# Hybrid decoder step on one core: fourteen input projections of the mixers as three products of rounded high and low parts, and the first tile's mixing moved forward

## The chip, the core and the metric

The kernel runs on one NeuronCore of one Trainium2 chip. The metric is the device time of one execution in microseconds, median of several runs; the kernel before has a median of 2032.25 us. The five engines are TensorE (PE in the profile, its weight loads PEld), VectorE (DVE), ScalarE (ACT), GpSimd (POOL) and SyncE (SP), which here only issues DMAs.

## What is computed

One inference step of a one-layer decoder on T = 592 tokens (16 meta tokens, 512 prompt tokens, 8 sample sequences of 8 tokens), all in float32. Cut to what matters here:

```python
q, k, v, g, f_lr, z, xbc, dt_raw = jnp.split(rmsnorm(h) @ w_in, offs, axis=-1)
gk   = log_sigmoid(f_lr @ w_gk2 + b_gk2) / 16          # decay of the linear attention
attn = jnp.sum(q[:, :, :, None] * exp(b_t - b_s) * k[:, :, None], axis=-1)   # inside chunks of 16
o    = attn @ v + (q * exp(b)) @ state                  # states follow each other, chunk by chunk
o_gla = rmsnorm(o) * silu(g)
xs, bm, cm = split(silu(causal_conv(xbc)))              # second mixer: state space, 8 heads
y    = rmsnorm((ssd(xs, dt, bm, cm) + d_skip * xs) * silu(z))
h    = h + concat(o_gla, y) @ w_out
h    = h + peer(rmsnorm(h))                             # 16384 experts, product keys, top 16 of 8 heads
```

## The kernel before, in words

Activations lie transposed, features on the 128 partitions and tokens along the row. The program is written out by hand, engine by engine; each engine runs its own list in order and waits on semaphores. There is no scheduler: the order in the source is the order on the engine.

**The mixers (the first 480 us or so).** `project(n, xn)` (L569) multiplies the n-th 128-feature block of `w_in` by the normed activations `xn`: 8 contraction tiles by 2 halves of 296 tokens, so 16 float32 matmuls. Blocks 0 and 1 are q, 2 and 3 are k, 4 to 7 are g, 8 to 11 are z, 12 to 19 are the convolution's input. A block's weights come by DMA into one of four slots of `ring` (`load_w`, L429), each load released when the product that held the slot is done (semaphore `proj_done`); behind each of the loads 4 to 11 SP also issues four 768 KB stores of zeros into the scratch table of gates. ACT copies each product from PSUM (`from_pair`, L1035, semaphore `proj_act`).

The PE runs products 0 to 3, turns k (L647), runs products 4 and 5, and then ten attention units u (two per token tile). A unit is `attn(u, 6 + u)`: sixteen steps, each one matmul of product 6 + u and one matmul with two columns (L662) that sums the decayed q times k over its features. Each unit's input `E_unit[u % 3]` is made by four engines in turn: DVE `decay_arg(u)` (L1387, L1388: difference of the running decays, capped at 0; it waits until unit u - 3 has been used), ACT `decay(u)` (L1073: exp), POOL a product with q (L1790), DVE `mult_k(u)` (L1394: times k), and then the PE. On ACT the exps stand between the copies of the products, with a table load at each change between exp and silu. In unit u DVE does `mult_k(u + 1)`, `decay_arg(u + 3)`, and after each odd unit `attn_matrix` (L385). ACT does, for n = 5 to 11, `from_pair(n)` and then `decay(n - 2)`.

After the units come the chunk-by-chunk states of the linear attention with products 15 to 19 between them, the state-space mixer (`pre`, L765 to L773, on the PE; `decays` L1499 and L1502, `weighted_x` L1511 to L1516 and `mixing` L1523 on DVE; then the outputs L824 on the PE), and the output projections.

**The experts (from about 484 us to the end).** 128 blocks of expert inputs and then 128 of expert outputs, each float32 operand split into a rounded high part and a low remainder in the type fp32r, which the PE takes in one pass: `split_product` (L875) multiplies high by high, high by low and low by high. ACT rounds (L1184), DVE subtracts (L1609).

Of the kernel before, what the change touches and what calls it, by code (L numbers as in the profile page):

```python
# [26 lines left out]
P = 128  # L27
# [19 lines left out]
N_PROJ = N_FEAT + KT + PH  # L47
GRP = 8
# [103 lines left out]
def build(nc, d, o):  # L152

    base = ExitStack()
    with base:
# [9 lines left out]

        h = sb(base, "h", [P, KT, T])
# [8 lines left out]
        prm = sb(base, "prm", [P, PARAM_N])  # L175
        sq = sb(base, "sq", [P, 2, T])
# [20 lines left out]
        mix_stack = ExitStack()  # L197
        mix = sb(mix_stack, "mix", [P, 8, T])
# [22 lines left out]
        khat = sb(gla, "khat", [P, TILES, GH * DK])  # L221
        tmp = sb(gla, "tmp", [P, 2, TILES, GH * DK])
        MT = sb(gla, "MT", [P, TILES, GH * P])
        S = sb(gla, "S", [P, 2, NP, DV])
        Ssm = sb(gla, "Ssm", [P, NSEQ, NP, DV])
# [9 lines left out]
        wv_sb = Ef[:, 0:KT * GH * DV].rearrange("p (k n) -> p k n", k=KT)  # L235
        gsq = Ef[:, 0:GH * T].rearrange("p (h t) -> p h t", h=GH)
# [178 lines left out]
        def _(sp):  # L415
# [26 lines left out]
            sp.dma_start(Ssm[:, :, :, :], d["s_gla"]).then_inc(sgla_loaded, 16)  # L442
            for n in range(12, N_FEAT):
                load_w(n)

# [65 lines left out]
            sp.wait_ge(xl_ready, KT)  # L511
# [38 lines left out]
        def _(pe):  # L550
# [85 lines left out]
            pe.wait_ge(v_copied, 4)  # L636
            project(0, xn, norm=0)
            pe.wait_ge(v_copied, TILES)
            pe.wait_ge(suf_exp, 3)
            for n in range(1, 4):  # L640
                project(n, xn)
# [8 lines left out]
            def attn(u, n=None):  # L650


                i, p = u // 2, u % 2
                if p == 0 and i >= 2:
                    pe.wait_ge(mt_ready, i - 1)
                pe.wait_ge(e_k, u + 1)
                src = E_unit[u % 3][:, 0:rows(i) * C].rearrange("p (t n) -> p t n", t=C)
                for t in range(C):
                    if n is not None:
                        project(n, xn, first=t, count=1)  # L660
                    out = bank[4 + i % 2][0:rows(i), p * 2 * C + t:p * 2 * C + C + t + 1:C]
                    mm = pe.matmul(out, src[:, t, :], cc("head2"), start=True, stop=True)  # L662
                mm.then_inc(attn_used, 1)


            project(4, xn)
            project(5, xn)
# [199 lines left out]
            def split_product(b, x, first=False):  # L867

                for k in range(KT):
                    if first:  # L870
                        pe.wait_ge(xl_ready, k + 1)
                    hi, lo = (usp[:, x, z, k * P:(k + 1) * P] for z in range(2))
                    for w, src in ((hi, xh), (hi, xl), (lo, xh)):
                        for y in range(2):
                            mm = pe.matmul(bank[b + y][:, 0:PHALF], w, src[:, k, y * PHALF:(y + 1) * PHALF],  # L875
                                           start=(k == 0 and w is hi and src is xh), stop=(k == KT - 1 and w is lo))
                return mm
# [24 lines left out]

            for n in range(N_FEAT + KT + 1, N_PROJ):
                pe.wait_ge(qlo_ready, n - N_FEAT - KT)
                wait_proj_evacuated(pe, n)
                split_product(2 * (n % 2), n % NU, n == N_FEAT + KT + 1).then_inc(proj_done, 1)
                if n == N_FEAT + KT + 1:
                    pe.wait_ge(hsm_keys_loaded, 32)
                if n >= N_FEAT + KT + 2:
                    first_scores(n - N_FEAT - KT - 2)  # L910
# [99 lines left out]
        def _(act):  # L1010
# [43 lines left out]
            act.wait_ge(rtok_ready, 2)  # L1054
            for i in range(TILES):
                act.wait_ge(v_done, i + 1)
                act.activation(V[0:rows(i), i, :], bank[[2, 3, 0, 1, 2][i]][0:rows(i), :], ACT.Copy,
                               scale=rtok[0:rows(i), i:i + 1]).then_inc(v_copied, 1)
# [16 lines left out]
            for n in range(15):  # L1075
                if n < 4:
                    from_pair(n, (qT if n < 2 else kT)[:, n % 2, :], scale=(DK ** -0.5 if n < 2 else 1.0))
                elif n < 12:
                    from_pair(n, (sg if n < 8 else sz)[:, n % 4, :], ACT.Silu)
                else:  # L1080
                    from_pair(n, h[:, n - 12, :])
                if n < 3:
# [219 lines left out]
        def _(dve):  # L1302
# [72 lines left out]
            dve.tensor_scalar(gk[:, :, :], tmp[:, 1, :, :], 1.0 / 16.0, None, ALU.mult).then_inc(gk_ready, 1)  # L1375
            dve.wait_ge(b_copied, 4)
# [19 lines left out]

            for u in range(3):
# [9 lines left out]

            dve.wait_ge(proj_act, 4)
            dve.wait_ge(khat_step, 1)
# [6 lines left out]
            mult_k(0)  # L1416
            for u in range(2 * TILES):
                if u + 1 < 2 * TILES:
                    mult_k(u + 1)
                if u + 3 < 2 * TILES:  # L1420
                    decay_arg(u + 3)
                if u % 2 == 1:
# [123 lines left out]
            for i in range(TILES):  # L1546
                r = rows(i)
                if i < 4:
                    decays(i + 1)
                mixing(i)  # L1550
# [32 lines left out]
            def low_x(k):  # L1583
                dve.wait_ge(xh_ready, k + 1)
# [197 lines left out]
        def _(pool):  # L1782
# [39 lines left out]
            for n in range(N_FEAT + KT + 1, N_PROJ):  # L1822
                pool.wait_ge(qhi_ready, n - N_FEAT - KT)
                if n == N_FEAT + KT + 3:
                    pool.wait_ge(xl_ready, KT)
# [124 lines left out]
```

## Time and profile before

| | |
|---|---|
| median of 3 runs (2029.19 to 2039.9) | 2032.25 us |
| the profiled execution | 2029.9 us |
| its span, first to last instruction | 2028.1 us |
| PE busy | 1991.8 us, 98% |
| DVE / ACT / POOL busy | 60% / 31% / 56% |
| mean granted PE clock, share of full speed | 0.988 |

The page gives, for one execution, the busy time of each engine, the chain of work that ended last, and groups of instructions by source line. The timeline lists an engine's instructions in order of start, neighbours of one kind merged: start in us, duration, engine, line, operation, output<-inputs, sizes, count, and in brackets how long the engine stood idle before and what released it. A float32 matmul shows as two records. Durations of matmuls reach from entry to drained result and overlap; the pitch from one start to the next is what a stream costs.

### The profile page before, as it was taken

Reading aid. Unit: us, or ns where it says so; the run is one execution under the profiler, and the core shown is the slowest. Engines: PE = TensorE matmul, PEld = TensorE weight load, DVE = VectorE, ACT = ScalarE, POOL = GpSimd, SP = SyncE. Lnnn points to the kernel's source line nnn. Section 1 sums busy time; section 2 is a strip of 40 time slices with the busy share of each in tenths; the row PEclk is TensorE's granted clock in tenths of the full one; section 3 lists DMA queues with packets and bytes.
Section 4 is the critical chain, followed back from the end, with each engine's and each line's share of the span. In section 5 each row is a group of like instructions: output and inputs, shape, how many; then the busy total and the mean of one; then the engine's idle time right before and its main releaser. Section 6 shows DMA issues by size and latency. Waiting matters only on the chain.

```text
span 2028.1 us, 31741 instructions
## 1 busy us (share of the span) xinstructions
PE 1991.8 (98%) x12557; PEld 1830.1 (90%) x12557; DVE 1216.5 (60%) x2243; ACT 633.6 (31%) x999; POOL 1138.3 (56%) x694
## 2 busy tenths in 40 slices
PE   8999999999999999999999999999999999999997
PEld 4678777868999999999999999998999999999996
DVE  4425365646898877788244331114677777777775
ACT  3325113323333233232323333223333333333332
POOL 0114210222367888888888888885566666666310
PEclk8999999899999999999999999999999999999999
DMA  3395103032245555555555555778999999999971
GB/s 151 108 337 198 32 32 89 1 111 101 96 122 122 130 115 130 121 129 127 127 130 126 120 124 121 171 169 281 333 328 325 326 329 325 326 325 328 330 259 48
DMA packets 233452, 365.28 MB, mean 180 GB/s; under 512 B 92129, under 2 KB 158194, under 8 KB 232690
## 3 DMA queue, kind: packets, MB, share of 16 engines
q1 hardware_dynamic: 154354, 294.37, 43.7%
q0 software_dynamic: 77824, 67.41, 17.0%
q10 hardware_dynamic: 1152, 1.84, 0.3%
q8 instruction: 81, 1.33, 0.3%
q14 instruction: 41, 0.34, 0.0%
HBM read 290.15 MB, written 73.38 MB: 179 GB/s over the span
## 4 chain that ended last, share of the span: by engine, by line
PE 95%; DVE 2%; ACT 1%; DMA 1%; SPq 0%; issue 0%; ACTq 0%; POOL 0%; DVEq 0%; POOLq 0%
PE bank L875 41%; PE bank L992 31%; PE bank L569 9%; PE bank L589 2%; PE bank L797 2%; PE bank L845 2%; PE bank L691 1%; PE bank L555 1%; PE bank L662 1%; PE bank L707 1%; PE bank L922 1%; PE bank L785 1%; PE bank L953 1%; PE bank L831 1%; DMA ring<-in_v 1%; PE bank L765 0%
## 5 line engine op out<-in xcount | busy, mean ns | idle before, releaser
L875 PE MATMUL bank<-xh,usp 128*128 128x288 f32 x4320 | 755.9, 296 | 1.4 <-DVE xl L1585 1.4
L1842 POOL DMA_INDIRECT gates_scratch<-gate_val,gate_at x384 | 674.1, 1755 | 132.6 <-issue 116.1
L875 PEld LDWEIGHTS bank<-xh,usp 128*128 128x128 f32 x4320 | 636.8, 189 | 4.0 <-DVE xl L1585 2.6
L992 PE MATMUL bank<-W,vsp 128*128 128x448 f32 x3072 | 623.1, 365 | 3.2 <-DVE W L1724 3.2
L992 PEld LDWEIGHTS bank<-W,vsp 128*128 128x128 f32 x3072 | 576.8, 188 | 49.1 <-issue 3.5
L875 PE MATMUL bank<-xl,usp 128*128 128x288 f32 x2160 | 462.5, 296 | 0.0
L875 PEld LDWEIGHTS bank<-xl,usp 128*128 128x128 f32 x2160 | 348.0, 189 | 0.0
L1609 DVE TENSOR_TENSOR usp<-ring,usp 128x1024 fp32r<-128x1024 f32 x120 | 146.6, 1221 | 335.1 <-ACT usp L1184 334.8
L1719 DVE TENSOR_TENSOR vsp<-ring,vsp 128x1024 fp32r<-128x1024 f32 x128 | 157.0, 1226 | 179.2 <-ACT vsp L1266 179.2
L1207 ACT ACTIVATE gl<-bank 128x288 f32<-128x288 f32 x256 | 91.3, 409 | 523.9 <-PE bank L875 523.8
L1861 POOL DMA_INDIRECT picked<-in_v,row_index x128 | 149.4, 1167 | 182.9 <-DVE acc L1738 162.4
L1868 POOL DMA_INDIRECT hid_b<-hidden_scratch,hid_index x128 | 190.1, 1485 | 55.3 <-issue 38.7
L569 PE MATMUL bank<-xn,ring 128*128 128x296 f32 x640 | 202.8, 439 | 0.0
L1266 ACT ACTIVATE vsp<-ring 128x1024 fp32r<-128x1024 f32 x128 | 135.6, 1060 | 183.3 <-PE bank L992 168.7
L1738 DVE SCALAR_TENSOR_TENSOR acc<-picked,w_b,acc 128x1024 f32<-128x1024 f32 x126 | 160.3, 1278 | 0.2
L1270 ACT ACTIVATE W<-sq 128x448 fp32r<-128x448 f32 x128 | 74.2, 580 | 233.9 <-DVE sq L1714 233.9
L1184 ACT ACTIVATE usp<-ring 128x1024 fp32r<-128x1024 f32 x128 | 136.0, 1063 | 14.4 <-DMA ring<-in_u 14.4
L569 PEld LDWEIGHTS bank<-xn,ring 128*128 128x128 f32 x640 | 107.8, 191 | 23.2 <-issue 7.3
L1790 POOL TENSOR_TENSOR E<-E,qT 128x2048 f32<-128x2048 f32 (+1 forms) x7 | 29.1, 4160 | 158.2 <-ACT qT L1035 91.4
L1714 DVE TENSOR_TENSOR sq<-xn,G 128x448 f32<-128x448 f32 x128 | 79.4, 620 | 5.1 <-DMA G<-gates_scratch 5.1
L1724 DVE TENSOR_TENSOR W<-sq,W 128x448 fp32r<-128x448 f32 x128 | 79.0, 617 | 1.3 <-ACT W L1270 1.2
L1814 POOL TENSOR_TENSOR Ct<-ecb,h 128x512 f32<-128x512 f32 (+1 forms) x10 | 13.5, 1369 | 81.7 <-ACT ecb L1143 81.7
(269 smaller groups left out, 1648.5 us busy)
## 6 DMA issues: line engine op xcount, KB each, us to landing
ring<-in_u SPq DMA_DIRECT2D x128, 512.0 KB, 3.8
ring<-in_v SPq DMA_DIRECT2D x128, 512.0 KB, 5.5
hidden_scratch<-gl SPq DMA_DIRECT2D x128, 288.0 KB, 2.1
xn<-hidden_scratch SPq DMA_DIRECT2D x128, 224.0 KB, 5.7
G<-gates_scratch SPq DMA_DIRECT2D x120, 224.0 KB, 4.8
gates_scratch<-zero SPq DMA_DIRECT2D x32, 768.0 KB, 8.7
ring<-in_wproj SPq DMA_DIRECT2D x36, 512.0 KB, 7.1
gates_scratch<-gate_val,gate_at POOLq DMA_INDIRECT x384, 4.1
```

The costliest lines, as they stand in the source:

```text
L569: mm = pe.matmul(bank[2 * (n % 2) + x][:, 0:half], ring[:, n % 4, k * P:(k + 1) * P], src[:, k, at + x * half:at + (x + 1) * half], start= ...
L875: mm = pe.matmul(bank[b + y][:, 0:PHALF], w, src[:, k, y * PHALF:(y + 1) * PHALF], start=(k == 0 and w is hi and src is xh), stop=(k == KT ...
L992: mm = pe.matmul(bank[(k + 4) % 8][:, 0:TA], w, W[:, n % 4, z, :], start=(n == 0 and w is hi and z == 0), stop=(n == NE - 1 and w is lo))
L1184: act.activation(usp[:, u_slot(j), 0, :], ring[:, j, :], ACT.Copy).then_inc(uhi_ready, 1)
L1207: ins = act.activation(gl[:, j, y * PHALF:(y + 1) * PHALF], bank[2 * (j % 2) + y][:, 0:PHALF], ACT.Gelu_apprx_tanh)
L1266: act.activation(vsp[:, n % 4, 0, :], ring[:, n % 4, :], ACT.Copy).then_inc(vhi_ready, 1)
L1609: dve.tensor_tensor(usp[:, u_slot(n), 1, :], ring[:, n % 4, :], usp[:, u_slot(n), 0, :].bitcast(F32), ALU.subtract).then_inc(ulo_ready, 1)
L1719: dve.tensor_tensor(vsp[:, n % 4, 1, :], ring[:, n % 4, :], vsp[:, n % 4, 0, :].bitcast(F32), ALU.subtract).then_inc(vlo_ready, 1)
L1738: ins = dve.scalar_tensor_tensor(acc[:, x % 2, :], picked[:, x % NROW, :], w_b[:, x:x + 1], acc[:, x % 2, :], ALU.mult, ALU.add)
L1842: pool.indirect_dma_start(gates_flat, bass.IndirectOffsetOnAxis(ap=gate_at[0:r, i, x:x + 1], axis=0), gate_val[0:r, i, hh, x - hh * TOPK:x ...
L1861: pool.indirect_dma_start(picked[:, x % NROW, :], None, rows_of_v, bass.IndirectOffsetOnAxis(ap=row_index[:, x:x + 1], axis=0)).then_inc(r ...
L1868: pool.indirect_dma_start(hid_b[:, x:x + 1], None, hid_flat, bass.IndirectOffsetOnAxis(ap=hid_index[:, x:x + 1], axis=0)).then_inc(picked_ ...
```

## The change

Products 1 to 14 become `project_split`: for each contraction tile and each half, three fp32r matmuls (high weights by high activations, high by low, low by high) instead of one float32 matmul. Product 0 and products 15 to 19 stay in float32. The rounded and low parts lie in the places of buffers that are dead by then: the activations' high part over `sq` and `h`, their low part over `mix`, a block's weights over `tmp` (odd n) and `Ssm` (even n), high and low side by side. ACT makes the high parts (`x_hi` eight times among its V copies; `split_w(n)` for each block, placed behind `from_pair(n - 2)`), DVE the low parts (eight times `x_lo` behind the last V product; `low_w(n)` fourteen times). The PE's product n waits for `low_w(n)`. The load of `Ssm` moves behind load 18. In the state-space mixer, the first tile's `mixing(0)` moves ahead of `decays(1)`.

```diff
+        def under(name, shape):
+            with ExitStack() as place:
+                return sb(place, name, shape, F32R)
+        h_rounded = under("h_rounded", [P, KT, T])
         h = sb(base, "h", [P, KT, T])
...
-            sp.dma_start(Ssm[:, :, :, :], d["s_gla"]).then_inc(sgla_loaded, 16)
             for n in range(12, N_FEAT):
                 load_w(n)
+                if n == N_SPLIT + 4:
+                    sp.dma_start(Ssm[:, :, :, :], d["s_gla"]).then_inc(sgla_loaded, 16)
...
+            def project_split(n, first=0, count=2 * KT):
+                if first == 0:
+                    pe.wait_ge(qlo_ready, n)
+                    wait_proj_evacuated(pe, n)
+                for m in range(first, first + count):
+                    k, x = m // 2, m % 2
+                    hi, lo = (split_slot[n % 2][:, z, k * P:(k + 1) * P] for z in range(2))
+                    for step, (w, src) in enumerate(((hi, x_hi(k)), (hi, x_lo(k)), (lo, x_hi(k)))):
+                        mm = pe.matmul(bank[2 * (n % 2) + x][:, 0:HALF], w, src[:, x * HALF:(x + 1) * HALF],
+                                       start=(k == 0 and step == 0), stop=(k == KT - 1 and step == 2))
+                if first + count == 2 * KT:
+                    mm.then_inc(proj_done, 1)
             project(0, xn, norm=0)
             pe.wait_ge(v_copied, TILES)
             pe.wait_ge(suf_exp, 3)
+            pe.wait_ge(xl_ready, KT)
             for n in range(1, 4):
-                project(n, xn)
+                project_split(n)
...
                     if n is not None:
-                        project(n, xn, first=t, count=1)
+                        project_split(n, first=t, count=1)
...
-            project(4, xn)
-            project(5, xn)
+            project_split(4)
+            project_split(5)
...
+            def split_w(n):
+                act.wait_ge(ring_loaded[n % 4], 16 * (n // 4 + 1))
+                act.activation(split_slot[n % 2][:, 0, :], ring[:, n % 4, :], ACT.Copy).then_inc(qhi_ready, 1)
             for i in range(TILES):
+                if i == 2:
+                    act.wait_ge(normed, KT)
+                    for k in range(KT):
+                        act.activation(x_hi(k), xn[:, k, :], ACT.Copy).then_inc(xh_ready, 1)
+                if i == 3:
+                    act.wait_ge(gk_ready, 1)
+                    split_w(1)
+                    split_w(2)
...
+                if 3 <= n + 2 <= N_SPLIT:
+                    split_w(n + 2)
                 if n < 3:
                     decay(n)
...
+            dve.wait_ge(v_done, TILES)
+            for k in range(KT):
+                dve.wait_ge(xh_ready, k + 1)
+                dve.tensor_tensor(x_lo(k), xn[:, k, :], x_hi(k).bitcast(F32), ALU.subtract).then_inc(xl_ready, 1)
             dve.wait_ge(b_copied, 4)
...
+            def low_w(n):
+                dve.wait_ge(qhi_ready, n)
+                dve.tensor_tensor(split_slot[n % 2][:, 1, :], ring[:, n % 4, :], split_slot[n % 2][:, 0, :].bitcast(F32),
+                                  ALU.subtract).then_inc(qlo_ready, 1)
+            low_w(1)
+            low_w(2)
             for u in range(3):
                 decay_arg(u)
...
+            low_w(3)
+            low_w(4)
             dve.wait_ge(proj_act, 4)
+            low_w(5)
...
             mult_k(0)
+            low_w(6)
             for u in range(2 * TILES):
                 if u + 1 < 2 * TILES:
                     mult_k(u + 1)
+                if u == 0:
+                    low_w(7)
                 if u + 3 < 2 * TILES:
                     decay_arg(u + 3)
+                if 8 + u <= N_SPLIT:
+                    low_w(8 + u)
                 if u % 2 == 1:
                     attn_matrix(dve, u // 2)
...
+                if i == 0:
+                    mixing(0)
                 if i < 4:
                     decays(i + 1)
-                mixing(i)
+                if i > 0:
+                    mixing(i)
```

The first place is DVE ahead of the attention units, from the end of the decays' logarithms (`tmp`, `qz`) to the two products of q with the decay (`qz<-qT,eb`) and what stands behind them. Before:

```order
L1375 TENSOR_SCALAR qz<-tmp 128x1280 [waits chain]
L1387 TENSOR_TENSOR E<-bT 128x2048 [waits v_copied,b_copied]
L1388 TENSOR_SCALAR E<-E 128x2048 [waits chain]
...
L1405 TENSOR_TENSOR qz<-qT,eb 64x2x592 [waits eb_ready,proj_act]
L1406 TENSOR_TENSOR qz<-qT,eb 64x2x592
L1412 TENSOR_TENSOR khat<-khat,bank 128x512 [waits suf_exp,khat_step,proj_act]
```

Now (`mix_rounded` is the activations' low part, `tmp_split` and `ssm_split` hold the parts of an odd and an even block):

```order
L1425 TENSOR_SCALAR qz<-tmp 128x1280 [waits chain]
L1429 TENSOR_TENSOR mix_rounded<-xn,sq_rounded 128x592 [waits xh_ready,v_done]
...
L1453 TENSOR_TENSOR tmp_split<-ring,tmp_split 128x1024 [waits qhi_ready,v_copied,b_copied]
L1453 TENSOR_TENSOR ssm_split<-ring,ssm_split 128x1024 [waits qhi_ready]
L1441 TENSOR_TENSOR E<-bT 128x2048
L1442 TENSOR_SCALAR E<-E 128x2048 [waits chain]
...
L1466 TENSOR_TENSOR qz<-qT,eb 64x2x592 [waits eb_ready,proj_act]
L1467 TENSOR_TENSOR qz<-qT,eb 64x2x592
L1453 TENSOR_TENSOR tmp_split<-ring,tmp_split 128x1024 [waits qhi_ready]
L1453 TENSOR_TENSOR ssm_split<-ring,ssm_split 128x1024 [waits qhi_ready]
L1453 TENSOR_TENSOR tmp_split<-ring,tmp_split 128x1024 [waits qhi_ready,proj_act]
L1476 TENSOR_TENSOR khat<-khat,bank 128x512 [waits suf_exp,khat_step]
```

Ten subtractions stand ahead of the first `decay_arg`, and the low parts of blocks 3 and 4 stand behind the two `qz` products, which wait for products 0 and 1.

The second place is one attention unit on DVE, an odd one. Before:

```order
L1394 TENSOR_TENSOR khm<-khm,kT 128x2048 [waits e_q]
L1387 TENSOR_TENSOR E<-bT 128x2048 [waits attn_used]
L1388 TENSOR_SCALAR E<-E 128x2048 [waits chain]
L385 TENSOR_TENSOR MT<-bank,cst 128x512 [waits attn_used]
L1394 TENSOR_TENSOR E<-E,kT 128x2048 [waits e_q]
```

Now:

```order
L1448 TENSOR_TENSOR khm<-khm,kT 128x2048 [waits e_q]
L1441 TENSOR_TENSOR E<-bT 128x2048 [waits attn_used]
L1442 TENSOR_SCALAR E<-E 128x2048 [waits chain]
L1453 TENSOR_TENSOR tmp_split<-ring,tmp_split 128x1024 [waits qhi_ready]
L405 TENSOR_TENSOR MT<-bank,cst 128x512 [waits attn_used]
L1448 TENSOR_TENSOR E<-E,kT 128x2048 [waits e_q]
```

Between `decay_arg` and the next `mult_k` there is now a subtraction that waits for ACT.

The third place is ACT in the same units. Before:

```order
L1073 ACTIVATE E<-E 128x2048 [waits e_arg]
L1035 ACT_TABLE_LOAD
L1035 ACTIVATE sg<-bank 128x296 [waits proj_done]
L1035 ACTIVATE sg<-bank 128x296
L1073 ACT_TABLE_LOAD
L1073 ACTIVATE khm<-khm 128x2048 [waits e_arg]
```

Now:

```order
L1121 ACTIVATE E<-E 128x2048 [waits e_arg]
L1071 ACT_TABLE_LOAD
L1071 ACTIVATE sg<-bank 128x296 [waits proj_done]
L1071 ACTIVATE sg<-bank 128x296
L1093 ACTIVATE tmp_split<-ring 128x1024 [waits ring_loaded1]
L1121 ACT_TABLE_LOAD
L1121 ACTIVATE khm<-khm 128x2048 [waits e_arg]
```

The rounding of a block's weights stands behind the exp, its table load and the copy, so it comes after `decay_arg` of the same unit.

## Rows read from the trace of the kernel before

**Rows 1.** The page: busy time by engine, and the last chain by engine.

```profile
PE 1991.8 (98%) x12557; PEld 1830.1 (90%) x12557; DVE 1216.5 (60%) x2243; ACT 633.6 (31%) x999; POOL 1138.3 (56%) x694
...
PE 95%; DVE 2%; ACT 1%; DMA 1%; SPq 0%; issue 0%; ACTq 0%; POOL 0%; DVEq 0%; POOLq 0%
```

**Rows 2.** Timeline of the PE: products 0 to 5, an attention unit's steps, the last unit.

```profile
75.44 32.06 PE L569 MATMUL bank<-xn,ring 128*128 128x296 f32 x128
...
109.52 16.61 PE L569 MATMUL bank<-xn,ring 128*128 128x296 f32 x66
...
126.11 0.74 PE L569 MATMUL bank<-xn,ring 128*128 128x296 f32 x2
...
126.83 0.74 PE L569 MATMUL bank<-xn,ring 128*128 128x296 f32 x2
...
228.66 2.43 PE L662 MATMUL bank<-cst,E 128*80 128x2 f32 x32
```

**Rows 3.** Timeline of the PE: six single-pass matmuls of the experts, first and seventh start.

```profile
495.18 0.69 PE L875 MATMUL bank<-xh,usp 128*128 128x288 f32 x4
...
495.97 0.69 PE L875 MATMUL bank<-xh,usp 128*128 128x288 f32 x4
```

**Rows 4.** Timeline of DVE, ACT and POOL in an attention unit.

```profile
137.11 2.29 DVE L1387 TENSOR_TENSOR E<-bT 128x2048 f32<-128x2048 f32 x1 [21.32 <-PE bank L662]
...
140.58 2.28 DVE L1394 TENSOR_TENSOR khm<-khm,kT 128x2048 f32<-128x2048 f32 x1
140.69 1.91 ACT L1073 ACTIVATE E<-E 128x2048 f32<-128x2048 f32 x1 [13.00 <-DVE E L1388]
...
142.68 3.86 POOL L1790 TENSOR_TENSOR E<-E,qT 128x2048 f32<-128x2048 f32 x1 [36.54 <-ACT E L1073]
143.92 0.73 ACT L1035 ACTIVATE sg<-bank 128x296 f32<-128x296 f32 x2
...
152.12 0.68 DVE L385 TENSOR_TENSOR MT<-bank,cst 128x512 f32<-128x512 f32 x1
```

**Rows 5.** The page's costliest groups: rounding and low part of one expert block.

```profile
L1609 DVE TENSOR_TENSOR usp<-ring,usp 128x1024 fp32r<-128x1024 f32 x120 | 146.6, 1221 | 335.1 <-ACT usp L1184 334.8
...
L1184 ACT ACTIVATE usp<-ring 128x1024 fp32r<-128x1024 f32 x128 | 136.0, 1063 | 14.4 <-DMA ring<-in_u 14.4
```

**Rows 6.** Timeline: DVE operations that meet POOL products, at two places.

```profile
92.34 1.38 DVE L1405 TENSOR_TENSOR qz<-qT,eb 64x1184 f32<-64x1184 f32 x1 [4.06 <-ACT qT L1035]
92.39 9.98 POOL L1790 TENSOR_TENSOR E<-E,qT 128x2048 f32<-128x2048 f32 x2 [91.38 <-ACT qT L1035]
...
93.74 4.93 DVE L1406 TENSOR_TENSOR qz<-qT,eb 64x1184 f32<-64x1184 f32 x1
...
349.71 2.50 POOL L1814 TENSOR_TENSOR Ct<-ecb,h 128x512 f32<-128x512 f32 x2 [58.30 <-ACT ecb L1143]
349.74 1.27 DVE L1513 TENSOR_TENSOR cum<-cum,dt 128x8 f32<-128x8 f32 x1 [0.77 <-ACT cum L1146]
```

**Rows 7.** Timeline: last V copy on ACT, first decay on DVE.

```profile
71.24 0.68 ACT L1057 ACTIVATE V<-bank,rtok 80x512 f32<-80x512 f32 x1 [6.18 <-PE bank L589]
...
75.24 2.29 DVE L1387 TENSOR_TENSOR E<-bT 128x2048 f32<-128x2048 f32 x1 [18.76 <-ACT bT L1062]
```

**Rows 8.** Timeline: the first tile of the state-space mixer.

```profile
351.04 1.72 DVE L1516 TENSOR_TENSOR XW<-xtok,cum 128x512 f32<-128x512 f32 x1
...
354.96 1.27 DVE L1523 TENSOR_TENSOR L<-L,bank 128x512 f32<-128x512 f32 x2
...
356.29 0.64 PE L824 MATMUL bank<-L,Xd 128*64 128x128 f32 x4 [2.64 <-DVE L L1523]
```

**Rows 9.** Windows of 2 us of the PE: start:end length, busy (instructions), PEclk, DMA share, GB/s.

```profile
356.00:358.00 2.00, 1.71 (x17) 0.60 0.00 0
358.00:360.00 2.00, 2.00 (x20) 0.55 0.00 0
```

**Rows 10.** DMA loads of projection weights (L429): issue to landing.

```profile
DMA to landing us min/median/max: 3.4/7.2/12.0
```

More of the change, by code:

```diff
@@ L47 @@
 N_PROJ = N_FEAT + KT + PH
+N_SPLIT = 14
 GRP = 8
@@ L175, in build @@
         prm = sb(base, "prm", [P, PARAM_N])
+        sq_rounded = under("sq_rounded", [P, 2, T])
         sq = sb(base, "sq", [P, 2, T])
@@ L197, in build @@
         mix_stack = ExitStack()
+        mix_rounded = under("mix_rounded", [P, KT, T])
         mix = sb(mix_stack, "mix", [P, 8, T])
@@ L221, in build @@
         khat = sb(gla, "khat", [P, TILES, GH * DK])
+        tmp_split = under("tmp_split", [P, 2, D])
         tmp = sb(gla, "tmp", [P, 2, TILES, GH * DK])
@@ L224, in build @@
         S = sb(gla, "S", [P, 2, NP, DV])
+        ssm_split = under("ssm_split", [P, 2, D])
         Ssm = sb(gla, "Ssm", [P, NSEQ, NP, DV])
@@ L235, in build, with x_hi, x_lo @@
         wv_sb = Ef[:, 0:KT * GH * DV].rearrange("p (k n) -> p k n", k=KT)
+        split_slot = [ssm_split, tmp_split]
+        def x_hi(k):
+            return sq_rounded[:, k, :] if k < 2 else h_rounded[:, k, :]
+        def x_lo(k):
+            return mix_rounded[:, k, :]
         gsq = Ef[:, 0:GH * T].rearrange("p (h t) -> p h t", h=GH)
@@ L510, in _ @@
                 sp.dma_start(gates_dram[part, :, TS:TA].rearrange("n p t -> p n t"), stage[:, part, :]).then_inc(gate_stored, 16)
-            sp.wait_ge(xl_ready, KT)
+            sp.wait_ge(xl_ready, 2 * KT)
             def load_gates(n):
@@ L870, in split_product @@
                     if first:
-                        pe.wait_ge(xl_ready, k + 1)
+                        pe.wait_ge(xl_ready, KT + k + 1)
                     hi, lo = (usp[:, x, z, k * P:(k + 1) * P] for z in range(2))
@@ L903, in _ @@
             for n in range(N_FEAT + KT + 1, N_PROJ):
-                pe.wait_ge(qlo_ready, n - N_FEAT - KT)
+                pe.wait_ge(qlo_ready, N_SPLIT + n - N_FEAT - KT)
                 wait_proj_evacuated(pe, n)
@@ L1583, in low_x @@
             def low_x(k):
-                dve.wait_ge(xh_ready, k + 1)
+                dve.wait_ge(xh_ready, KT + k + 1)
                 dve.tensor_tensor(xl[:, k, :], xn[:, k, META:T], xh[:, k, :].bitcast(F32), ALU.subtract).then_inc(xl_ready, 1)
@@ L1822, in _ @@
             for n in range(N_FEAT + KT + 1, N_PROJ):
-                pool.wait_ge(qhi_ready, n - N_FEAT - KT)
+                pool.wait_ge(qhi_ready, N_SPLIT + n - N_FEAT - KT)
                 if n == N_FEAT + KT + 3:
-                    pool.wait_ge(xl_ready, KT)
+                    pool.wait_ge(xl_ready, 2 * KT)
                 pool.tensor_tensor(usp[:, n % NU, 1, :], ring[:, n % 4, :], usp[:, n % NU, 0, :].bitcast(F32), ALU.subtract
```

## The prediction

> **What bounds the kernel now.** I read the page first: the PE is busy for 98% of the span, and 95% of the chain that ended last runs through it [rows 1]. So a change pays where it shortens the PE's list, as long as no other engine then keeps the PE waiting. The timelines of the stage that is edited come next. A float32 product of 16 matmuls takes 32.06 / 4 = 8.02 us, 0.501 us a matmul, and the PE goes through products 0 to 3 and then 4 and 5 without a gap [rows 2]. In an attention unit a step (one matmul of the product, one of two columns) has a pitch of 126.83 - 126.11 = 0.72 us, so a unit takes 11.5 us. The first unit begins at 109.52 + 32 x 0.501 = 125.6 and ends at 137.1, and the ninth (unit 8) ends at 228.66, where the last unit without a product begins [rows 2]. In [rows 4] the reader is to see who works beside a unit: DVE prepares the next input (3.6 us to the start of the exp), ACT takes the exp, a table load and the copy, POOL multiplies. No PE wait stands in that stage before. These engines matter once work is put between their links.
>
> **The change, part by part.** The sum goes against the profiled execution, 2029.9 us (span 2028.1 and 1.8 around it); the median of the three runs is 2.35 us higher, which I leave out.
>
> *The matmuls.* Six single-pass matmuls with 288 columns take 495.97 - 495.18 = 0.79 us, 0.133 each [rows 3]; eight columns more at 2.4 GHz make it 0.136. Three are 0.41 us against 0.501, so a product falls from 8.0 to 6.5 us, and a step in a unit from 0.72 to 0.63, a unit from 11.5 to 10.1. If nothing else moved, 14 x 16 x 0.092 = 20.6 us would go.
>
> *The activations' parts.* Eight rounded copies on ACT lie between its V copies, which wait for the PE by 6.2 us [rows 7], and cost nothing; without that cover they would be about 5 us. The eight subtractions on DVE wait for the last V product (71.2 [rows 7]) and take 8 x 0.73 (L1609 [rows 5] scaled to 592 elements): done at 77.1. Two weight subtractions at 1.22 [rows 5] follow, so the first `decay_arg` starts at 79.7 instead of 75.24 [rows 7]. Product 1 finds its parts ready when product 0 ends at 83.5. Products 1 and 2 end at 90.0 and 96.6, 3 us sooner.
>
> *The stall before product 3.* Its low part stands on DVE behind the two products of q with the decay, and these share something with POOL: where two DVE operations and two POOL products meet, they run strictly in turn. The second DVE one takes 4.93 us against 1.38 for its twin, and an operation of 8 elements takes 1.27 us when it begins behind a POOL product [rows 6]. A POOL product alone is (9.98 - 1.3 - 1.3) / 2 = 3.7. So from the copy of product 1 (90.9): POOL to 94.7, `qz` to 96.0 (its clears lie inside POOL's time), POOL to 99.7, second `qz` to 101.0. The third exp is ready at 96.6 + 0.9 (copy) + 1.06 (rounding) + 1.91 = 100.4, so POOL is next, to 104.7; then the low part, to 106.0. The PE idles from 96.6 to 106.1. After an idle of 2.64 us [rows 8] the granted clock was 0.60 and 0.55 over 4 us [rows 9], which is the lower level for most of it and 1.7 us of work lost; I take the same once here. Product 3 then ends at 114.4 instead of 107.5. Its copy, the turn of k and products 4 and 5 follow as before (2.07 us from 107.45 to 109.52 [rows 2], then 13.1), and the first unit begins at 129.5 and ends at 139.5: 2.4 later than before. The low end, with no turn lost to POOL, is a start of product 3 at 97; the nearest miss is DVE's low part ahead of POOL's third product, which fails by 0.6 us and would give back 3.7.
>
> *The loop in the units.* This is the largest term. In unit u + 1 `mult_k(u + 2)` now stands behind `low_w(8 + u)`, that waits for the rounding on ACT, that stands behind `from_pair(6 + u)` and the exp of u + 3, and that waits for `decay_arg(u + 3)` on DVE. Before, no such ring existed. From the start D of `decay_arg`, by [rows 4]: exp from 3.58 to 5.5; POOL's product to 5.6 + 3.7 = 9.3 (the 3.86 there contain the end of a DVE product); on ACT table load and copy to 7.5 and rounding to 8.6. The subtraction has two SBUF inputs like the ones of rows 6, so it waits for POOL until 9.3 and ends at 10.6; `mult_k` takes 2.28, so 12.9; after an odd unit L385 adds 0.6, so 13.5. The next `decay_arg` starts there, and the unit that `mult_k` feeds too. Both are longer than the PE's 10.1 and than the 11.5 of before. The unit after the first starts at once (its input is ready). The next five starts follow at the ring's pace, 12.9, 13.5, 12.9, 13.5 and 12.9 us after the one before; then the short tile's operations (1280 elements in place of 2048) give some 11.0, and the last two units are the PE's, 10.1 and 9.5. Together 96.4 us from the end of unit 0 to the end of unit 8, against 228.66 - 137.1 = 91.6: 4.8 lost. The ring's price is bounded from below by its length without the wait for POOL (8.6 + 1.2 + 2.3 = 12.1 and 12.7) and from above by the rival on the clock.
>
> By the Trainium skill (SBUF — State Buffer, section "SBUF: two separate sides") VectorE and GpSimd share a port pair as an exclusive lock: an operation of VectorE with two SBUF inputs and a GpSimd operation that reads SBUF shut each other out for a whole instruction. The trace agrees, with 1.27 us for 8 elements [rows 6]; no row of before shows the weight subtraction itself beside a POOL product. By that rule the sum is the one below, without it that of the first rival.
>
> *DMA.* Loads land 3.4 to 12.0 us after their issue [rows 10]. A unit of 13 us needs one load, and `split_w` asks for it about two units after its slot is free, so loads stay hidden; if the zeros ahead of them ran late, a load would cost the part over 12. `Ssm` is first read at the samples' states some 70 us later: nothing.
>
> *The mixing.* The PE waits 2.64 us for `mixing(0)` [rows 8]. DVE is free for it at 351.04 + 1.72 = 352.76, and I take its exp as done by then, since nothing but DVE is named for the wait; it now ends at 354.0 instead of 356.2. The masks of tile 1 come 0.5 us later, which the PE's next 7 us of work hide. I take 2.0 of the 2.2.
>
> **Sum:** +2.4 at the start of the units, +4.8 in them, -2.0 in the mixing: +5.2, 2035 us. That is within 0.5% of before, about what a measurement of this kernel can tell from no change (10 us).
>
> **The rivals.**
> *The DVE subtractions do not wait for POOL.* For it: no row shows just this operation beside a POOL product. Against: the turns in [rows 6]. Then product 3 starts at 97 and needs no colder clock (unit 0 ends 10.9 sooner, at 128.6), the ring is 12.1 and 12.7, and unit 8 ends at 221.2, 7.5 before the old time. With the mixing 2020 us.
> *Only the PE's list counts.* The saving is 20.6 + 2.0, 2007 us. For it: in [rows 4] DVE works for some 6 us of a unit of 11.5, ACT for some 4. Against: the ring, which is an order of waits and not a load.
> *The clock falls in the units and stays down (slower).* The PE now idles about 3 us in each of five units, and after 2.64 us its clock was at the lower level [rows 8, 9]. A fall like that one costs 1.7 us and makes a unit 11.8, still inside the ring's 12.9, so it is hidden. It decides when the lower level lasts over 5.6 us of a unit. If it holds through, a unit takes 20.2 instead of 13.1, five of them 35 us: 2070. Against: in [rows 9] the clock was back before 360.
>
> **How the numbers follow.** The ring with the waits for POOL: 0.65 (own range 2029 to 2043, from the port's order before product 3 and the clock). No waits for POOL: 0.13. The PE alone: 0.07. The clock: 0.15, spread from 2038 to 2070. Predicted 2035. The range goes from 2020, the first rival, to 2049, halfway into the clock's case; it leaves out the PE's case and the upper half of the clock's. Faster by over 0.5% (under 2022 against the median): the PE's case and half of the first rival, 0.13. Slower by over 0.5%: most of the clock's case and a little of the forecast's upper end, 0.16. Within: 0.71.
>
> **What would show it.** Right: one PE wait of 9 us on a low part before product 3; starts of the units 13 us apart, with a PE wait of 3 us on `mult_k`; weight subtractions near 2.0 us in the units against 1.2 elsewhere; the 2.64 us before L824 under 1. Wrong: units 10 us apart (the ring does not close), subtractions at 1.2 throughout (no wait for POOL), or a granted clock near 0.5 across whole units.

## The result and the profile after

The changed kernel took 2081.69 us (median of 4 runs, 2078.76 to 2090.89), the kernel before 2035.89 us (median of 4): a ratio of 1.0233, 95% interval 1.0196 to 1.0269. It is slower, where 2035 us was forecast. The profiled execution took 2083.8 us (span 2081.7), 53.9 us more than the profiled one of before. One execution each of e1 (2053.16 us) and e6 (2048.28 us), over 1.5% above the fastest of its kernel, is left out of the ratios given below.

The page, first the busy time, then the granted clock in 40 slices of 52 us, then the last chain:

```profile
PE 2033.1 (98%) x12781; PEld 1898.8 (91%) x12781; DVE 1251.2 (60%) x2265; ACT 651.8 (31%) x1021; POOL 1131.1 (54%) x694
...
PEclk9995579999999999999999999999999999999999
...
PE 93%; DVE 4%; ACT 1%; DMA 1%; issue 0%; SPq 0%; DVEq 0%; ACTq 0%
```

Against [rows 1] the PE is busy for 41 us more, though its list should have become 20.6 us shorter; its share of the span is 98% as before. The reason stands in the second row: three slices at 5 and 7 tenths of the clock. The PE stood idle for some 12 us more (48.6 us against 36.3), nearly all of it in two waits; the other 41 us are work that went more slowly. The timeline of the PE, with its idle time in brackets, shows where that begins:

```profile
105.39 0.62 PE L667 MATMUL bank<-sq_rounded,tmp_split 128*128 128x296 f32 x1 [9.14 <-DVE tmp_split L1453]
...
114.99 1.28 PE L683 MATMUL bank<-cst,kT 128*128 128x128 f32 x10 [0.91 <-ACT kT L1071]
...
152.25 0.41 PE L667 MATMUL bank<-sq_rounded,ssm_split 128*128 128x296 f32 x1 [2.67 <-DVE khm L1448]
...
152.90 0.38 PE L667 MATMUL bank<-sq_rounded,ssm_split 128*128 128x296 f32 x1
...
153.53 0.38 PE L667 MATMUL bank<-sq_rounded,ssm_split 128*128 128x296 f32 x1
...
257.03 0.59 PE L667 MATMUL bank<-h_rounded,tmp_split 128*128 128x296 f32 x1
...
258.20 0.59 PE L667 MATMUL bank<-h_rounded,tmp_split 128*128 128x296 f32 x1
...
280.25 4.41 PE L698 MATMUL bank<-cst,E 128*80 128x2 f32 x32
...
406.77 0.45 PE L860 MATMUL bank<-L,Xd 128*64 128x128 f32 x4 [0.37 <-DVE L L1592]
```

From the start of the products to 280 there are only two waits of over 1 us: the 9.14 us before product 3 and one of 2.67 us on `mult_k`, before unit 2. Right behind it a step of a unit still takes 153.53 - 152.90 = 0.63 us; from 154 on it takes 1.17 us (258.20 - 257.03), where the kernel before needed 0.72 [rows 2]. Unit 8 ends at 280.25 instead of 228.66 [rows 2], 51.6 us later. The windows of the PE (start:end length, busy (instructions), granted clock, DMA share, GB/s):

```profile
104.00:108.00 4.00, 2.61 (x10) 0.50 0.99 303
108.00:112.00 4.00, 4.00 (x25) 0.81 1.08 370
112.00:116.00 4.00, 3.09 (x25) 1.00 1.05 347
148.00:152.00 4.00, 1.58 (x14) 1.00 1.00 283
152.00:156.00 4.00, 3.75 (x22) 0.74 1.09 372
156.00:160.00 4.00, 4.00 (x20) 0.50 1.10 353
276.00:280.00 4.00, 4.00 (x19) 0.50 0.00 0
288.00:292.00 4.00, 4.00 (x20) 0.69 0.00 0
292.00:296.00 4.00, 4.00 (x32) 1.00 0.00 0
```

After the long idle before product 3 the clock is back by 110, some 4 us into the product. After the short idle at 150 it falls too, at 154, to its lower level (0.50 is 1.2 GHz, 1.00 is 2.4 GHz), and stays there for some 136 us although the PE then has no gap at all. DMA traffic does not hold it down: at 276 to 280 there is none. It rises at 290, when the float32 products of the next stage (from 287.55) have begun. At 1.2 GHz a unit takes 18.7 us (five starts of DVE's decay from 169.71 to 244.37 stand 18.66 to 18.67 apart), longer than the ring of 13 us, so the ring never shows again. The ring's one appearance, in the timeline of DVE, ACT and POOL:

```profile
100.61 4.72 DVE L1453 TENSOR_TENSOR tmp_split<-ring,tmp_split 128x1024 fp32r<-128x1024 f32 x1
105.25 1.21 DVE L1453 TENSOR_TENSOR ssm_split<-ring,ssm_split 128x1024 fp32r<-128x1024 f32 x1
...
139.48 2.29 DVE L1441 TENSOR_TENSOR E<-bT 128x2048 f32<-128x2048 f32 x1 [7.05 <-PE bank L698]
...
145.06 3.85 POOL L1862 TENSOR_TENSOR E<-E,qT 128x2048 f32<-128x2048 f32 x1 [40.81 <-ACT E L1121]
146.90 1.06 ACT L1093 ACTIVATE ssm_split<-ring 128x1024 fp32r<-128x1024 f32 x1
148.00 1.99 DVE L1453 TENSOR_TENSOR ssm_split<-ring,ssm_split 128x1024 fp32r<-128x1024 f32 x1 [4.97 <-ACT ssm_split L1093]
149.91 2.28 DVE L1448 TENSOR_TENSOR khm<-khm,kT 128x2048 f32<-128x2048 f32 x1
152.11 2.28 DVE L1441 TENSOR_TENSOR E<-bT 128x2048 f32<-128x2048 f32 x1
```

Decay at 139.48, POOL's product to 148.91, the low part behind it (1.99 us, and 4.72 before product 3, against 1.21 without POOL), `mult_k` to 152.19, then the PE and, at 152.11, the next decay: 12.6 us from decay to decay, about as worked out. What followed was not.

A table of places, in us, serves all runs (from the timelines and the groups of lines). The experts' first product is the best single measure of the change: behind it the kernels are alike, but their second expert products take 623 to 626 us in some profiles (623.1 in that of before) and 635 to 637 in others (636.8 in e9, 635.3 in e3, both without the split).

| kernel | first two-column matmul of the units | last one | experts' first product |
|---|---|---|---|
| before | 126.0 | 230.9 | 484.5 |
| changed | 129.7 | 284.4 | 536.0 |
| e1 early rounding | 130.1 | 223.6 | 478.5 |
| e2 one float32 product | 130.0 | 279.4 | 529.5 |
| e3 before, with a wait | 123.6 | 236.6 | 490.4 |
| e4 product, then sums | 136.5 | 242.7 | 496.0 |
| e5 low part behind | 129.6 | 225.1 | 476.8 |
| e6 both waits gone | 119.4 | 214.9 | 469.8 |
| e8 three units float32 | 119.7 | 216.2 | 471.5 |
| e9 mixing alone | 125.4 | 230.3 | 486.5 |

### The profile page after: what moved, and what is told of

The parts are those of the page before. It is cut to its first block, busy times and chain, and to the rows that moved or that the text cites. A ratio compares the mean times of both kernels' runs of the same rounds, so it can differ in the third digit from the quotient of the medians.

```text
span 2081.7 us, 32237 instructions
## 1 busy us (share of the span) xinstructions
PE 2033.1 (98%) x12781; PEld 1898.8 (91%) x12781; DVE 1251.2 (60%) x2265; ACT 651.8 (31%) x1021; POOL 1131.1 (54%) x694
## 4 chain that ended last, share of the span: by engine, by line
PE 93%; DVE 4%; ACT 1%; DMA 1%; issue 0%; SPq 0%; DVEq 0%; ACTq 0%
PE bank L911 40%; PE bank L1028 30%; PE bank L667 6%; PE bank L590 2%; PE bank L610 2%; PE bank L881 2%; PE bank L698 1%; PE bank L833 1%; PE bank L727 1%; PE bank L576 1%; PE bank L743 1%; PE bank L958 1%; DMA ring<-in_v 1%; PE bank L989 1%; PE bank L821 0%
## 5 line engine op out<-in xcount | busy, mean ns | idle before, releaser
L1028 PE MATMUL bank<-W,vsp 128*128 128x448 f32 x3072 | 624.5, 366 | 4.0 <-DVE W L1796 4.0
L667 PE MATMUL bank<-h_rounded,ssm_split 128*128 128x296 f32 x168 | 67.8, 432 | 0.0
L667 PE MATMUL bank<-h_rounded,tmp_split 128*128 128x296 f32 x168 | 60.9, 403 | 0.0
L590 PE MATMUL bank<-xn,ring 128*128 128x296 f32 x192 | 59.8, 440 | 0.0
```

Source lines behind the costliest of these rows:

```text
L590: mm = pe.matmul(bank[2 * (n % 2) + x][:, 0:half], ring[:, n % 4, k * P:(k + 1) * P], src[:, k, at + x * half:at + (x + 1) * half], start= ...
L667: mm = pe.matmul(bank[2 * (n % 2) + x][:, 0:HALF], w, src[:, x * HALF:(x + 1) * HALF], start=(k == 0 and step == 0), stop=(k == KT - 1 and ...
L1028: mm = pe.matmul(bank[(k + 4) % 8][:, 0:TA], w, W[:, n % 4, z, :], start=(n == 0 and w is hi and z == 0), stop=(n == NE - 1 and w is lo))
```

## Experiments

The theory after the result: the one wait of 2.67 us lowers the clock, and the units' new mix (three single-pass products of 296 columns, two matmuls of two columns, and so on) keeps the level it meets; it cannot raise the clock again, which the float32 mix can. The rivals: the new mix cannot hold the high level at all, wait or no wait; or any wait in the units lowers it for good, whatever the matmuls are.

### e1: take the wait out

ACT's rounding for product 8 + u needs only that unit u is over. It is moved ahead of the exp, so DVE finds it ready behind the decay:

```diff
-                if 3 <= n + 2 <= N_SPLIT:
+                if 3 <= n + 2 <= 7:
                     split_w(n + 2)
                 if n < 3:
                     decay(n)
                 elif 5 <= n < 12:
+                    act.wait_ge(proj_done, n + 2)
+                    split_w(n + 3)
                     decay(n - 2)
```

> ACT rounds the next weights ahead of the exp instead of behind the copy, so that the low part on DVE no longer stands behind the exp, the table load and POOL's product; nothing else is changed. Theory (the one wait of 2.67 us at 149.6 lowers the clock, and the units' mix of split products and two-column matmuls keeps whichever level it meets): no wait on DVE in the units, granted clock 1.0 throughout, units 10.1 us apart, unit 8 ends near 220 instead of 280, 2021 us in all. Rival (the mix itself cannot hold the higher level, and the clock would have fallen at 154 without a wait): no waits, but the clock falls to 0.5 some 25 us into the units all the same, units near 19 us, about 2080 us.

Measured: 2025.55 us for the profiled execution, a median of 2031.73 over ten, ratio to before 0.9975 (0.9939 to 1.0012). The rows of the PE and of its windows around the one wait that is left in the units, then DVE's low part:

```profile
201.83 0.41 PE L667 MATMUL bank<-sq_rounded,tmp_split 128*128 128x296 f32 x1 [0.92 <-DVE E L1450]
...
143.38 1.22 DVE L1455 TENSOR_TENSOR ssm_split<-ring,ssm_split 128x1024 fp32r<-128x1024 f32 x1
...
190.62 4.28 DVE L1443 TENSOR_TENSOR khm<-bT 128x1280 f32<-128x1280 f32 x1 [0.78 <-PE bank L698]
```

```profile
200.00:202.00 2.00, 1.08 (x10) 1.00 0.19 16
202.00:204.00 2.00, 2.00 (x17) 1.00 0.69 246
```

The clock is 1.0 through all units, without a float32 product among them; the last two-column matmul starts at 223.6 instead of 284.4. So the mix holds the high level, and the rival falls. The gain is not safe, though: DVE and POOL, which take turns, are now nearly full. POOL's product (128x2048) takes 5.0 to 5.6 us, the decay grows from 2.29 us to 4.77 over five units and still takes 4.28 with 1280 elements, and before unit 7 the PE waits 0.92 us. Over the ten executions the mean granted clock was 0.985 to 0.987 in the six of 2021.1 to 2033.1 us, and 0.975 to 0.978 in the four of 2034.5 to 2053.2: there, I take it, the clock fell in the units, which is not shown, as there is no profile of such an execution.

### e2: one float32 product in the slow stretch

Only the PE's matmuls of product 10 change; ACT and DVE still make its parts.

```diff
-                        project_split(n, first=t, count=1)
+                        if n in (10,):
+                            if t == 0:
+                                pe.wait_ge(qlo_ready, n)
+                            project(n, xn, first=t, count=1)
+                        else:
+                            project_split(n, first=t, count=1)
```

> Only TensorE's matmuls of product 10 (beside unit 4) go back to float32; ACT and DVE still round and subtract for it. Theory (the split mix cannot raise the clock, the float32 mix can): the clock comes back to 1.0 a few us into unit 4; unit 4 takes some 14 us instead of 20, and the ring's wait returns behind it (about 2 us), after which the clock falls again; some 6 to 15 us less than the changed kernel in all, 2070 to 2078. Rival (the level is held down by something other than the kind of matmul, as the length of the stage or the other engines): clock 0.5 through unit 4 as well, which then takes 23 us; 2087.

Measured: the last two-column matmul starts 5.0 us earlier than in the changed kernel, the experts 6.5 us earlier. The whole execution took 2089.47 us, because its second expert products fell on the longer of the two times (636.8 us against 624.5 in the profile of the changed kernel). Windows of the PE, and the first matmul of unit 6:

```profile
200.00:202.00 2.00, 2.00 (x6) 0.50 0.00 0
202.00:204.00 2.00, 2.00 (x13) 0.93 0.00 0
204.00:206.00 2.00, 2.00 (x13) 1.00 0.00 0
216.00:218.00 2.00, 1.79 (x15) 1.00 0.00 0
218.00:220.00 2.00, 0.00 (x0) 0.84 0.45 133
220.00:222.00 2.00, 1.49 (x6) 0.50 0.35 137
```

```profile
220.51 0.58 PE L667 MATMUL bank<-sq_rounded,ssm_split 128*128 128x296 f32 x1 [2.71 <-DVE E L1453]
```

The float32 unit begins at 189.92 and the clock is back at 202.1, 12 us into it. Unit 5, split again, runs at 1.0 and so outruns the ring: a wait of 2.71 us, the clock falls, and it stays at 0.5 to the end of the units. The same history twice in one execution: the float32 mix raises, the split mix keeps, a wait of 2.7 us lowers. The return took 12 us where I expected "a few", so the float32 unit took 17.6 us (189.92 to 207.51) and not some 14.

### e3: the kernel before, with a wait

```diff
+                if u == 1:
+                    dve.memset(h[:, :, :], 0.0)
+                    dve.memset(mix[:, :, :], 0.0)
+                    dve.memset(sq[:, :, :], 0.0)
                 if u + 1 < 2 * TILES:
                     mult_k(u + 1)
```

> The kernel before, with three clears of dead buffers on DVE (about 9 us) ahead of the product with k for unit 2, so that TensorE idles once there, as in the changed kernel, while its units are float32. Theory (an idle of 2 to 4 us lowers the clock in any mix, but float32 units raise it again): an idle of 2 to 4 us before unit 2, granted clock 0.5 for some 4 to 10 us behind it, then 1.0; 4 to 9 us slower than before. Rival (a wait in the units lowers the clock for the rest of the stage whatever the matmuls are): clock 0.5 to the end of the units, some 80 us slower than before.

```profile
151.59 1.35 PE L569 MATMUL bank<-xn,ring 128*128 128x296 f32 x2 [5.36 <-DVE khm L1394]
```

```profile
154.00:156.00 2.00, 2.00 (x8) 0.50 1.09 369
156.00:158.00 2.00, 2.00 (x9) 0.79 1.04 326
158.00:160.00 2.00, 2.00 (x13) 1.00 1.02 247
```

The idle came out at 5.36 us, twice that of the changed kernel. The clock fell, and was back at 156.8, 5 us after work had begun again. The experts start 5.9 us later than before. A wait alone does not keep the clock down: it takes the split units.

### e4: the product first, the two-column matmuls behind it

```diff
-                for t in range(C):
-                    if n is not None:
-                        project_split(n, first=t, count=1)
+                if n is not None:
+                    project_split(n)
+                for t in range(C):
                     out = bank[4 + i % 2][0:rows(i), p * 2 * C + t:p * 2 * C + C + t + 1:C]
```

> The changed kernel, with each unit's split product first (48 matmuls in a row) and its 32 two-column matmuls behind it, instead of interleaved step by step. The amount of work is the same. Theory (it is the two-column matmuls between the products that keep the clock down): after the first wait the clock falls, but comes back to 1.0 within each product, as it did in product 3 (4 us behind the idle of 9.14 us); units at the ring's pace of 13 us, 2035 to 2045 us. Rival (single-pass products cannot raise the clock in this stage at all): 0.5 to the end, 2080 us or more.

Measured: 2042.80 us; the experts start at 496.0 against 536.0. The 32 two-column matmuls of unit 0, and the windows of the PE from there into unit 1:

```profile
136.48 3.63 PE L698 MATMUL bank<-cst,E 128*128 128x2 f32 x32
```

```profile
138.00:140.00 2.00, 2.00 (x20) 1.00 0.91 200
140.00:142.00 2.00, 2.00 (x13) 0.81 1.01 366
142.00:144.00 2.00, 2.00 (x10) 0.50 1.11 378
144.00:146.00 2.00, 2.00 (x14) 0.84 1.07 358
146.00:148.00 2.00, 2.00 (x16) 1.00 1.10 373
```

The clock comes back within the products, as the theory has it: here some 3 us after it fell, with single-pass products alone. So the single-pass products by themselves do not keep it down; with the two-column matmuls between them they do. One thing was not expected: the clock now falls without any wait, right behind the 32 two-column matmuls in a row (the first wait of this stage comes at 152). Grouping makes the kernel recover, and makes it need to.

### e5: a wait of under 1 us

DVE's low part goes behind the next `mult_k`; ACT's order stays that of the changed kernel.

```diff
                     mult_k(u + 1)
-                if u == 0:
-                    low_w(7)
+                if 7 + u <= N_SPLIT:
+                    low_w(7 + u)
                 if u + 3 < 2 * TILES:
                     decay_arg(u + 3)
-                if 8 + u <= N_SPLIT:
-                    low_w(8 + u)
```

> The changed kernel, with each unit's low part on DVE behind the product with k of the next unit instead of ahead of it; ACT's order is as in the changed kernel. By the durations this leaves a wait of 0.8 to 1.4 us for the low part in each unit (ring of 10.9 to 11.5 us against TensorE's 10.1). Theory (the first wait of 2.67 us is what lowers the clock; waits of about 1 us do not): clock 1.0 in the units, unit 8 ends near 227, 2026 to 2030 us. Rival (any repeated wait lowers it): the clock falls to 0.5 in the first units and stays, 2070 to 2085 us.

```profile
161.08 0.37 PE L667 MATMUL bank<-sq_rounded,tmp_split 128*128 128x296 f32 x1 [0.79 <-issue]
```

```profile
160.00:164.00 4.00, 3.21 (x27) 1.00 1.02 321
```

Five waits of 0.34 to 0.79 us (0.8 to 1.4 were expected), one before each of units 2 to 6, and the clock stays at 1.0. Median 2025.01 us, ratio 0.9969 (0.9932 to 1.0006). Two lines of DVE's program in another order are worth some 57 us against the changed kernel; neither e1 nor e5 can be told from the kernel before, as both intervals include 1. What separates e5 from the changed kernel, as far as the traces show, is the length of the idle: in the profiled executions waits of up to 0.8 us (0.92 in e1) left the clock alone, 2.67 and 2.71 lowered it. Between them lie only waits behind 32 two-column matmuls in a row (1.83 us at 190.7 in e4, 1.6 us behind the last unit), where the clock fell too; by e4 it can fall there without a wait.

### e6, e8: both waits gone, and three float32 units

e6 is e1 with the low parts of products 3 and 4 ahead of the two products of q with the decay:

```diff
+            low_w(3)
+            low_w(4)
             dve.wait_ge(proj_act, 2)
             dve.wait_ge(eb_ready, 1)
...
-            low_w(3)
-            low_w(4)
             dve.wait_ge(proj_act, 4)
```

> The early rounding of the run before, and on DVE the low parts of products 3 and 4 ahead of the two products of q with the decay. Theory: product 3 starts at 96 without the idle of 9 us, the first unit starts near 118.6 instead of 129.3, the clock stays at 1.0, unit 8 ends near 209 to 212; 9 to 11 us less than the early rounding alone, about 2013. Rival (DVE only passes the wait on, to the turn of k, the product with k or the next low part): product 3 starts at 96, but the first units wait for their inputs, gain under 4 us, about 2020. If a wait of over 2 us is left in the units, the clock falls and the time is over 2040.

e8 is e6 with products 8, 10 and 12 in float32, and no parts made for them:

```diff
+PLAIN = (8, 10, 12)
+SPLITS = [n for n in range(1, N_LAST + 1) if n not in PLAIN]
...
-                        project_split(n, first=t, count=1)
+                        if n in PLAIN:
+                            project(n, xn, first=t, count=1)
+                        else:
+                            project_split(n, first=t, count=1)
...
-                if 8 + u <= N_SPLIT:
+                if 8 + u in SPLITS:
                     low_w(8 + u)
```

> Both waits gone as in the run beside it, and products 8, 10 and 12 (in units 2, 4 and 6) left in float32 with no parts made for them. The point: a float32 unit gives DVE and POOL, which take turns, 11.5 us instead of 10.1, and raises the clock again if it has fallen. Theory: 3 x 1.4 = 4 us more than the run with all fourteen split if its clock stays up, about 2017, and less spread between executions; 2020 to 2030 us less than that run in executions where its clock falls. Rival (the spread between executions has nothing to do with the clock in the units): the same spread as the run beside it, 4 us higher.

Measured: e6 2018.07 us (ratio 0.9922, 0.9894 to 0.9950), e8 2015.00 us (0.9915, 0.9895 to 0.9936). e6's first unit starts 10.3 us earlier than the changed kernel's, its experts at 469.8; the low part simply changed places with work that had time. It keeps four waits of 0.5 to 0.7 us in the units, the longest

```profile
171.61 0.37 PE L667 MATMUL bank<-sq_rounded,tmp_split 128*128 128x296 f32 x1 [0.70 <-ACT sz L1071]
```

and nine of its ten executions spread from 2007.6 to 2028.2 us. The tenth took 2048.28 us at a mean granted clock of 0.974, like the four of e1; it has no profile, so whether a longer wait came back in its units is open. e8 has no wait in the units at all; one window over all of them reads

```profile
120.00:216.00 96.00, 96.00 (x696) 1.00 0.68 222
```

and its four executions lie between 2010.6 and 2019.5 us. It is slower than e6 by 1.3 us up to the last unit, less than the 4 us expected, because e6 has its waits there (2.4 us in all). The medians don't tell the two apart; e8 is the one I would keep, for the slack that a float32 unit gives DVE and POOL. That it spreads less than e6 because of this slack is not shown by four executions. Both are faster than the kernel before, by some 0.8% with both intervals below 1, and than the changed one.

### e9: the mixing alone

```diff
+                if i == 0:
+                    mixing(0)
                 if i < 4:
                     decays(i + 1)
-                mixing(i)
+                if i > 0:
+                    mixing(i)
```

> The kernel before with the first tile's mixing ahead of the decays of tile 1, and nothing else. Theory: the wait of 2.64 us before the first product of that tile falls to 0.4, a second wait of 0.6 comes at the next tile; the clock's dip behind it (0.60 and 0.55 over 4 us) goes too; 1.5 to 3 us less than before in the stretch from the last attention unit to the experts. Rival (the wait only moves to the masks of tile 1): the same stretch as long as before.

```profile
355.59 0.45 PE L824 MATMUL bank<-L,Xd 128*64 128x128 f32 x4 [0.37 <-DVE L L1523]
...
365.93 0.45 PE L824 MATMUL bank<-L,Xd 128*64 128x128 f32 x4 [0.59 <-DVE L L1523]
...
419.63 7.62 DVE L1324 SCALAR_TENSOR_TENSOR mix<-mix,prm,sq 128x592 f32<-128x592 f32 x4
...
416.61 6.16 POOL L1824 TENSOR_TENSOR h<-h,E 128x592 f32<-128x592 f32 x4
...
427.35 7.29 PE L845 MATMUL bank<-mix,ring 128*128 128x296 f32 x16 [3.33 <-issue]
```

The wait of 2.64 us [rows 8] becomes 0.37 and 0.59, and the last part of that stage before the second norm (line 555) starts 410.56 - 232.1 = 178.5 us behind the first product with V, against 413.90 - 232.7 = 181.2 before: 2.7 us gained. The clock's dip of [rows 9] was expected to go with it; instead a dip as long lies some 12 us earlier, at 345 to 348. Then it is given back. DVE's four operations of the norm take 7.62 us beside POOL's additions, against 5.34 in the trace of before, the PE, which starts 0.1 us after they end, waits 3.33 us instead of 1.04, and its clock falls (7.29 us for 16 matmuls that took 4.23 before). The experts start 2.0 us later than before. The changed kernel has the same wait (3.1 us), and e1, e4 and e6 as well (3.1 to 3.5), while e2, e5 and e8, with the same mixing, have 1.5, 1.2 and 0.8. It depends on how DVE and POOL happen to meet; that the moved mixing makes it likelier is open, with one trace of each.

## Why the prediction was wrong, by its own steps

- **What bounds the kernel, and the edits' prices: right.** At the full clock a step takes 0.63 us, as said, and a split product 6.6 (product 2, 89.5 to 96.1; 6.5 said). Products 1 and 2 end at 89.5 and 96.1 (90.0 and 96.6 said).
- **The stall before product 3: right, mechanism and size.** 9.14 us (9.5 said), the end at 105.4 (106.1), low part 4.72 us behind POOL; the first unit starts at 129.3 (129.5), and the clock came back within product 3.
- **The ring: right where it showed, once.** 12.6 us from decay to decay (12.9), a wait of 2.67 us (about 3), a subtraction of 1.99 (near 2.0). The rival without waits for POOL falls with these rows. The rule of the Trainium skill (SBUF — State Buffer, section "SBUF: two separate sides"), that a two-input instruction of DVE and a POOL instruction that reads SBUF shut each other out for the whole instruction, agrees with them.
- **The clock in the units: the step that failed.** The text priced the fall behind the ring's wait at 1.7 us, hidden in the ring, and gave the case that it stays down 0.15, "Against: in [rows 9] the clock was back before 360." These rows are a stretch with another mix of matmuls. In its place the runs showed that the return depends on what the PE runs afterwards: float32 products beside two-column matmuls bring the clock back (e3 and e2), split products alone too (product 3, e4), split products with two-column matmuls between them don't (126 us of units in the changed kernel; 37 us, and again 55, in e2). Why this mix does not is open. The trace of before had the split product's parts nowhere beside two-column matmuls, so it could not show this; but the edit put just that mix into nine units, and this was reason to let the price of a fall reach as far as the units do.
- **That rival's own price: too small.** It had five slow units of 20.2 us, 2070 us. A slow unit takes 18.7 us, but the clock stayed down through all of units 2 to 8 and into the next stage. From 152.25 to 280.25, seven units take 128.0 us; the forecast had the end of unit 8 at 139.5 + 96.4 = 235.9, so 44.4 of the missing 48.7 us (2083.8 - 2035.1) lie here.
- **The mixing: right at its place, lost behind it.** The wait fell as said. From the end of unit 8 to the experts the changed kernel takes 255.75 us and the one before 255.84: the 2.0 us are gone, 1.9 us of the error. Up to the second norm (461.76, and 413.90 before) this stretch is 3.7 us shorter, behind it 3.7 longer: a wait of 3.1 us instead of 1.0, and a fall of the clock at 478. The experts themselves took 2.1 us longer in this execution (1545.7 against 1543.6), nearly all of the rest.

## What to carry to other kernels

A shorter list for the PE is worth only what the others can keep up with, and a wait can cost far more than itself (2.67 us here): look what the PE runs after it. Behind float32 products beside two-column matmuls, or single-pass products in a row, the clock was back after 3 to 12 us; with two-column matmuls between single-pass products the lower clock lasted to the end of the stage, and one wait cost some 44 us. So when products are made cheaper, first take out the waits that this uncovers (here by moving one rounding or two subtractions). Leaving a few long units where the helpers are full, as in e8, is worth a try, though four executions don't show that it helps.

## What the hardware showed that was not expected

- The level of the clock has a memory in this stage: the same list of matmuls, units 2 to 6, ran without an idle at 1.0 in e1 (149.88 to 200.91, 51 us) and, but for the first 2 us, at 0.5 in the changed kernel (152.25 to 244.20, 92 us).
- The fall has no fixed place behind a wait: the same wait of 2.67 us before unit 2 was followed by it 1.7 us after work began again in the changed kernel (154), and inside the wait in e2 (151).
- The clock can fall without an idle around thirty-two two-column matmuls in a row (e4: about 1 us after their end at 140.1; e6: at 213.9, while those of the last unit still ran).
- The time to come back differs: about 3 us after the fall in e4, and from the start of work 4 us in product 3, 5 in e3 and 12 in e2. What sets it stays open.
- An instruction of DVE grows with the POOL product that it meets, up to 4.72 us for 1.21. With DVE and POOL nearly full (e1) such meetings grow from unit to unit (decay 2.29, 2.61, 3.54, 3.86 and 4.77 us) until the PE waits.
